# Search steps interleaved with other work, and expert gates in slabs of sixteen keys

## The chip, the cores and the metric

The kernel runs on one core of a Trainium2 chip. The metric is the device time of one execution in microseconds, lower is better. Three runs of the kernel before gave 3557.41, 3567.39 and 3569.17 us; the median is 3567.39.

## The reference, cut to what matters

The program is a two-layer model on 512 tokens of width 1024. Each layer has a mixer (an RWKV-7 half and an S5 half), a cross attention to 256 memory rows, and a PEER layer: a feed-forward layer with 16384 experts, of which each token takes 16 for each of 8 heads. The change touches the PEER layer alone:

```python
def peer_ffn(h, wq, keys, u_tab, v_tab):          # for each block of 128 tokens
    q = (hc @ wq).reshape(128, 8, 2, 128)
    sc = jnp.einsum('thcd,hckd->thck', q, keys)    # scores of 128 keys in each of 2 halves
    s1, i1 = lax.top_k(sc[:, :, 0], 16)
    s2, i2 = lax.top_k(sc[:, :, 1], 16)
    cand = s1[..., :, None] + s2[..., None, :]     # 256 pairs
    top, pos = lax.top_k(cand, 16)
    eidx = take(i1 * 128 + i2, pos)                # expert numbers
    gate = jax.nn.softmax(top, axis=-1)
    act = jax.nn.gelu(jnp.einsum('thkd,td->thk', u_tab[eidx], hc))
    return jnp.einsum('thk,thkd->td', gate * act, v_tab[eidx])
```

All data are float32.

## The kernel before, in words

`peer(pg, layer)` (L2358) treats 352 of the 512 tokens densely: it multiplies them with all 16384 rows of both expert tables, an up tile of 128 experts at a time, and weighs the results with a gate that is zero for experts that were not chosen. The other tokens go by gathering: 128 tokens on the 128 partitions, with 128 chosen experts each, plus 32 extra tokens of which each has four partitions and 32 chosen rows a partition. So GpSimd gathers 160 groups of 128 rows of the first table (512 KB each, `ROWS` = 160), VectorE takes the dot product of each with the tokens (a "row", L2881), and later 128 groups of the second table are added up, again one instruction of VectorE each.

A product in float32 is made of three products in a rounded format: ScalarE writes the high half of a tile (`split_high`, L216), VectorE the low half (`split_low`, L221), and `product` (L224) issues three matmuls for each of 8 planes, so 24 a tile. There are three buffers for raw tiles, three for high halves and three for low ones (`NRAW`, `NSPLIT`), so that ScalarE can make the high half of tile m only when the product of tile m - 3 is done, and SyncE's `load(m)` waits for the low half of tile m - 3.

The order of the tiles is `STREAM` (L2339): 144 of them, 16 query tiles of 512 columns (`q`) and 128 up tiles of 352 columns (`u`). Each engine runs its own list in order, and what stands ahead of an instruction on its engine holds it.

1. **Search**, eight slots, one a head. While TensorE does 12 tiles (10 up and the 2 query tiles of the next head) and the scores, VectorE runs `search(hd)` (L2892): two `top16` calls over 128 keys for two blocks of tokens and both halves, pair sums (`PAIRS`, 64 pairs that alone can be among the best 16), a third `top16` over them, arithmetic on the positions that finds which of the four groups of pairs a winner is in, masks (`hit`) that turn positions into key numbers, sums over them, and the row numbers that GpSimd waits for (`rows_found`). Steps that depend on one another on VectorE are joined by `link` (L95): the instruction increments a semaphore and the next one waits for it. At ten places of a slot, and twice more behind it, `split_and_row` puts one low half and, from the second head on, a row or two: 14 rows a slot (`ROWS_BY_HEAD`).
2. **Bridge**, six tiles, in which the gates are formed and transposed.
3. **Spreading**, 22 groups of 16 tokens with one or two up tiles each (`GROUP_AT`): VectorE makes one-hot matrices, TensorE multiplies them into dense gates, ScalarE copies them to `spill`, and `store_gates(n)` on SyncE (L2478) writes the 1 MB of a group to memory, laid out by slabs of `SLAB` = 8 keys, so in runs of 512 bytes. 0.75 rows a group.
4. **Tile loop**, the last 12 up tiles. VectorE has 135 low halves done when it enters its part of the loop (near L3085); each step is a low half and rows up to a count that grows by `ROWS_BY_TILE` = 2 a tile.
5. **Down**, 128 tiles of the second table. `weigh(e)` (L3091) multiplies the up results of a tile (kept in SBUF for the last 18 keys, else loaded back by `load_act`) with its gates from a slab, ScalarE and VectorE split both, TensorE multiplies. A slab (8 keys, 1408 KB) is loaded by one transfer, `load_slab(s)` (L2483), into one of two buffers. In the first 8 tiles (`DOTS_UNTIL`) VectorE finishes the rows of the first table that are left; the rows of the second table are spread over the later tiles. The order of the tiles is `DOWN`.

GpSimd issues the gathers (L2564) in the order `ROW_ORDER`, six buffers ahead of VectorE, and at the counts in `PART_GATES_AT` and `PART_GATHER_AT` the transfers for the extra tokens.

## Time and profile before

| what | value |
|---|---|
| median of 3 runs | 3567.39 us |
| profiled execution | 3566.76 us, its span 3564.8 us |
| TensorE busy | 3416.0 us, 96% of the span |
| VectorE busy | 2986.1 us, 84% |
| ScalarE busy | 1363.2 us, 38% |
| moved by DMA | 922.20 MB, mean 259 GB/s |

Busy time is the sum of an engine's instructions with overlaps counted once. The trace gives the start of each instruction; the distance between the starts of two tiles' first matmuls is what a tile really costs. "Granted clock" is the share of TensorE's full speed in a stretch.

### The profile page before, as it was taken

The page shows a single profiled execution, that of the slowest core. Times are in us where ns is not written, and L with a number is a line of the kernel's source. Part 1 is how long each engine was busy: PE and PEld are TensorE (multiplying, and loading weights), DVE is VectorE, ACT ScalarE, POOL GpSimd, SP SyncE. Part 2 cuts the span into 40 slices and gives each one's busy share as a digit, 9 for nine tenths or more (in the row PEclk, how much of TensorE's full clock was granted, in tenths as well). Part 3 has the DMA queues.
Part 4 walks back from the last instruction along what each step waited for, and adds up shares of the span by engine and source line. Part 5 has one row for each costly group of instructions (what it writes and reads, how often), then busy time and mean ns, then how long its engine had stood idle before and what let it go on. Part 6 is the DMA issues. An engine that isn't in the chain of part 4 may idle for free. (4 is left out here: it accounts for less than half of the span.)

```text
span 3564.8 us, 68150 instructions
## 1 busy us (share of the span) xinstructions
PE 3416.0 (96%) x27550; PEld 3116.0 (87%) x27550; DVE 2986.1 (84%) x5697; ACT 1363.2 (38%) x2116; POOL 989.6 (28%) x756
## 2 busy tenths in 40 slices
PE   8899899999999989999999989999999999999998
PEld 5678677999899989999997877789998999999997
DVE  8687575899999978888888757489999997888887
ACT  3541343433334433333344135343333443333333
POOL 2000000133343245445510000002334324543452
PEclk9999999999999999999999999999999999999999
DMA  7820431699899999999962043259989999999995
GB/s 236 302 95 23 132 113 60 192 292 310 291 358 319 345 336 359 369 376 368 366 220 83 20 121 119 65 155 299 311 297 348 317 349 327 374 383 384 363 367 205
DMA packets 392170, 922.20 MB, mean 259 GB/s; under 512 B 33968, under 2 KB 211248, under 8 KB 385072
## 3 DMA queue, kind: packets, MB, share of 16 engines
q1 hardware_dynamic: 298672, 582.20, 48.7%
q0 software_dynamic: 93184, 335.65, 25.1%
q8 instruction: 217, 3.56, 0.4%
q14 instruction: 97, 0.79, 0.1%
HBM read 802.51 MB, written 113.05 MB: 257 GB/s over the span
## 5 line engine op out<-in xcount | busy, mean ns | idle before, releaser
L2564 POOL DMA_INDIRECT row<-in_peer_u_rows,row_at x320 | 414.6, 1296 | 739.0 <-DVE row L2881 629.3
L228 PE MATMUL peer_ps<-peer_h_high,tile_high 128*128 128x352 f32 (+1 forms) x1504 | 498.0, 331 | 17.0 <-DVE tile_low L221 14.1
L229 PE MATMUL peer_ps<-peer_h_low,tile_high 128*128 128x352 f32 (+1 forms) x1504 | 492.2, 327 | 0.0
L230 PE MATMUL peer_ps<-peer_h_high,tile_low 128*128 128x352 f32 (+1 forms) x1504 | 491.7, 327 | 0.0
L221 DVE TENSOR_TENSOR tile_low<-peer_tile,tile_high 128x1024 fp32r<-128x1024 f32 x362 | 441.4, 1220 | 30.9 <-ACT tile_high L216 27.4
L228 PE MATMUL peer_ps<-gate_high,tile_high 128*128 128x352 f32 x1360 | 442.6, 325 | 9.6 <-DVE tile_low L221 9.3
L230 PE MATMUL peer_ps<-gate_high,tile_low 128*128 128x352 f32 x1360 | 441.3, 325 | 0.0
L229 PE MATMUL peer_ps<-gate_low,tile_high 128*128 128x352 f32 x1360 | 439.5, 323 | 0.0
L216 ACT ACTIVATE tile_high<-peer_tile 128x1024 fp32r<-128x1024 f32 x362 | 379.5, 1049 | 14.1 <-DMA peer_tile<-in_peer_u 14.1
L216 ACT ACTIVATE gate_high<-weighed 128x352 fp32r<-128x352 f32 x256 | 127.8, 499 | 643.6 <-DMA peer_tile<-in_peer_v 332.6
L2881 DVE SCALAR_TENSOR_TENSOR row<-row,h_own 128x1024 f32<-128x1024 f32 x256 | 307.4, 1219 | 23.1 <-DMA row<-in_peer_u_rows,row_at 22.9
L2716 ACT ACTIVATE up_act<-peer_ps 128x352 f32<-128x352 f32 x220 | 102.5, 466 | 575.6 <-PE peer_ps L230 294.1
L228 PEld LDWEIGHTS peer_ps<-peer_h_high,tile_high 128*128 128x128 f32 x1504 | 282.7, 188 | 38.7 <-DVE tile_low L221 23.8
L2564 POOL DMA_INDIRECT late_row<-in_peer_v,row_at x130 | 223.5, 1719 | 239.6 <-DVE h_own L2887 221.1
L230 PEld LDWEIGHTS peer_ps<-peer_h_high,tile_low 128*128 128x128 f32 x1504 | 283.2, 188 | 3.9
L229 PEld LDWEIGHTS peer_ps<-peer_h_low,tile_high 128*128 128x128 f32 x1504 | 283.1, 188 | 3.9
L2564 POOL DMA_INDIRECT row<-in_peer_v,row_at x126 | 215.7, 1712 | 216.3 <-DVE h_own L2887 201.7
L228 PEld LDWEIGHTS peer_ps<-gate_high,tile_high 128*128 128x128 f32 x1360 | 255.3, 188 | 16.0 <-DVE tile_low L221 15.4
L228 PE MATMUL peer_ps<-peer_h_high,peer_tile_high 128*128 128x352 f32 (+1 forms) x736 | 249.9, 339 | 18.0 <-DVE peer_tile_low L221 12.4
L230 PEld LDWEIGHTS peer_ps<-gate_high,tile_low 128*128 128x128 f32 x1360 | 256.3, 188 | 0.0
L229 PEld LDWEIGHTS peer_ps<-gate_low,tile_high 128*128 128x128 f32 x1360 | 255.6, 188 | 0.0
L221 DVE TENSOR_TENSOR gate_low<-weighed,gate_high 128x352 fp32r<-128x352 f32 x256 | 133.0, 520 | 135.2 <-ACT tile_high L216 92.6
(571 smaller groups left out, 8179.0 us busy)
## 6 DMA issues: line engine op xcount, KB each, us to landing
peer_tile<-in_peer_u SPq DMA_DIRECT2D x256, 512.0 KB, 5.4
peer_tile<-in_peer_v SPq DMA_DIRECT2D x256, 512.0 KB, 6.2
gates<-gates_out SPq DMA_DIRECT2D x44, 1024.0 KB, 9.1
gates_in<-gates SPq DMA_DIRECT2D x32, 1408.0 KB, 10.4
acts<-up_act SPq DMA_DIRECT2D x220, 176.0 KB, 5.6
act_in<-acts SPq DMA_DIRECT2D x220, 176.0 KB, 6.1
in_w<-in_w_in SPq DMA_DIRECT2D x32, 512.0 KB, 3.6
peer_tile<-in_peer_wq SPq DMA_DIRECT2D x32, 512.0 KB, 5.1
```

The source lines that it names most:

```text
L216: return act.activation(out, value, ACT.Copy)
L221: return dve.tensor_tensor(out, value, high.bitcast(F32), ALU.subtract)
L228: pe.matmul(out, wh, mh, start=first, stop=False)
L229: pe.matmul(out, wh, ml, start=False, stop=False)
L230: return pe.matmul(out, wl, mh, start=False, stop=last)
L2564: pool.indirect_dma_start(row_of(n)[:, :], None, table, bass.IndirectOffsetOnAxis(ap=row_at[:, row_col(n):row_col(n) + 1], axis=0)) \
L2716: act.activation(up[i % NUP][:, :], ps[m % NPS][:, 0:TD], ACT.Gelu_apprx_tanh).then_inc(taken.sem, 1)
L2881: last = dve.scalar_tensor_tensor(out=x, in0=x, scalar=1.0, in1=(h_own if j < OWN else h_extra)[:, :], op0=ALU.mult, op1=ALU.mult, accum_o ...
```

## The change

Five edits, all in `peer` and its constants.

- **Order of the search.** `link` gives way to `mark` (increment, and remember the count) and `until` (wait for a count). Between a producer and its consumer stands `gap(hd, share)`, which issues low halves and rows in step with its share of 29 (`GAPS`). In `top16` the four replaces go ahead of the four finds. The slot has the same 12 low halves (9 in the first) and 16 rows for 14.
- **Pairs.** `PAIRS` becomes (0,1,16), (1,2,8), (3,4,4), (7,8,2), (15,1,1): four groups of 16 and one of 1, 65 in all. The group number of a position is then a shift by 4 bits (`fours`, a constant buffer) in place of three comparisons and a cast.
- **Rows.** 16 a head, 0.75 a group, 1.5 a tile (2.0 before); the counts at which GpSimd issues the transfers for the extra tokens move with them.
- **Slabs.** `SLAB` is 16: stored runs are 1 KB. A slab has four pieces by token groups (`PIECES`: 6, 6, 5 and 5 groups of 16 tokens). The last sixteen keys are taken as two half slabs first (`TAKEN`), the other seven slabs whole. `PIECES_AT` says behind which tile load SyncE issues each piece. The second slab buffer lies over the plane `h_high` (address 41376), so its first load waits until all up products are done. The number of kept up results stays 18.
- **Rooms and waits.** `late_row3` moves to 208864, and GpSimd waits for all gate stores before the first gather of the second table.

```diff
-ROWS_BY_HEAD, ROWS_BY_GROUP, ROWS_BY_TILE = 14, 0.75, 2.0
+ROWS_BY_HEAD, ROWS_BY_GROUP, ROWS_BY_TILE = 16, 0.75, 1.5
-PAIRS = ((0, 1, 16), (1, 3, 8), (4, 4, 4), (8, 8, 1))
+PAIRS = ((0, 1, 16), (1, 2, 8), (3, 4, 4), (7, 8, 2), (15, 1, 1))
+GAPS = 29
-SLAB, NSLAB, NACT = 8, 2, 4
+SLAB, NSLAB, NACT = 16, 2, 4
+PIECES = ((0, 6), (6, 12), (12, 17), (17, TD // SPILL))
-KEPT_LATE, KEPT_EARLY = SLAB, 10
+KEPT_LATE, KEPT_EARLY = SLAB // 2, 10
+TAKEN = [(SLABS - 1, SLAB // 2, SLAB // 2), (SLABS - 1, 0, SLAB // 2), *((s, 0, SLAB) for s in (SLABS - 2, *range(SLABS - 2)))]
+PIECES_AT = [(0, 2, 4, 5), (4, 5, 6, 7), *([TAKEN_AT[s - 1] + 1 + j for j in ((2, 5, 8, 11) if TAKEN[s - 1][2] == SLAB else (0, 2, 4, 5))]
+                                           for s in range(2, len(TAKEN)))]
...
-        slabs = [buf(f"gates_in{b}", [P, TD // SPILL, SLAB * SPILL]) for b in range(NSLAB)]
+        slabs = [buf("gates_in0", [P, TD // SPILL, SLAB * SPILL]), pg.placed("gates_in1", [P, TD // SPILL, SLAB * SPILL], F32, 41376)]
...
-            def load_slab(s):
+            def load_slab(s, piece):
                 if s >= NSLAB:
-                    sp.wait_ge(weighed.sem, weighed.at(SLAB * (s - NSLAB + 1)))
+                    sp.wait_ge(weighed.sem, weighed.at(TAKEN_AT[s - NSLAB + 1]))
+                elif s:
+                    sp.wait_ge(summed.sem, summed.at(UPS))
                 else:
                     for b in range(2):
                         sp.wait_ge(gates_stored[b].sem, gates_stored[b].at(16 * ((TD // SPILL + 1 - b) // 2)))
-                sp.dma_start(slabs[s % NSLAB][:, :, :], gates[DOWN[s * SLAB] // SLAB]) \
+                (at, first, some), groups = TAKEN[s], slice(*PIECES[piece])
+                sp.dma_start(slabs[s % NSLAB][:, groups, 0:some * SPILL], gates[at][:, groups, first * SPILL:(first + some) * SPILL]) \
...
-                if m == GROUP_AT[GROUPS] + late + 1:
-                    load_slab(0)
-                if m == UPS:
-                    load_slab(1)
+                if m - GROUP_AT[GROUPS] - late - 1 in PIECES_AT[0]:
+                    load_slab(0, PIECES_AT[0].index(m - GROUP_AT[GROUPS] - late - 1))
...
                 if n == ROWS:
                     pool.wait_ge(summed.sem, summed.at(UPS))
+                    for b in range(2):
+                        pool.wait_ge(gates_stored[b].sem, gates_stored[b].at(16 * ((TD // SPILL + 1 - b) // 2)))
...
+            def mark(ins):
+                vec_step.n += 1
+                ins.then_inc(vec_step.sem, 1)
+                return vec_step.n
+            def until(step):
+                dve.wait_ge(vec_step.sem, step)
+            def lows_of(hd):
+                return BRIDGE + 3 - (PH - 1 - hd) * (UPS_HEAD + 2) - slot_start[0]
+            def gap(hd, share):
+                gaps_done[0] += share
+                some = ROWS_BY_HEAD if hd else 0
+                both = (lows_of(hd) + some) * gaps_done[0] // GAPS
+                own_lows = min(both, (2 * lows_of(hd) * gaps_done[0] + GAPS) // (2 * GAPS))
+                lows(slot_start[0] + own_lows - done[0])
                 if hd:
+                    rows((hd - 1) * ROWS_BY_HEAD + both - own_lows)
+            def top16(some, hd, shares):
                 for x, r, v, a in some:
                     last = dve.max(v[:, 0:8], x)
-                link(last)
+                best_8 = mark(last)
+                gap(hd, shares[0])
+                until(best_8)
+                for x, r, v, a in some:
+                    last = dve.match_replace(out=r, in_to_replace=v[:, 0:8], in_values=x, imm_value=LOWEST)
+                replaced = mark(last)
                 for x, r, v, a in some:
                     dve.max_index(a[:, 0:8], v[:, 0:8], x)
-                    last = dve.match_replace(out=r, in_to_replace=v[:, 0:8], in_values=x, imm_value=LOWEST)
-                link(last)
-                split_and_row(hd)
+                gap(hd, shares[1])
+                until(replaced)
                 for x, r, v, a in some:
                     last = dve.max(v[:, 8:16], r)
-                link(last)
+                next_8 = mark(last)
+                gap(hd, shares[2])
+                until(next_8)
...
-                link(dve.tensor_copy(spotf[0][:, :, :], pos[:, :, :]))
-                link(dve.tensor_scalar(spotf[1][:, :, :], spotf[0][:, :, :], float(PAIR_AT[1]), None, ALU.is_ge))
-                link(dve.scalar_tensor_tensor(out=spotf[1][:, :, :], in0=spotf[0][:, :, :], scalar=float(PAIR_AT[2]),
-                                              in1=spotf[1][:, :, :], op0=ALU.is_ge, op1=ALU.add))
-                for _ in range(2):
-                    link(dve.scalar_tensor_tensor(out=spotf[1][:, :, :], in0=spotf[0][:, :, :], scalar=float(PAIR_AT[3]),
-                                                  in1=spotf[1][:, :, :], op0=ALU.is_ge, op1=ALU.add))
-                link(dve.tensor_copy(wide[:, :, :], spotf[1][:, :, :]))
+                block_known = mark(dve.tensor_tensor(wide[:, :, :], pos[:, :, :], fours[:, :, :], ALU.logical_shift_right))
...
                 for into in hits:
+                    gap(hd, 1)
+                    until(hits_known)
```

The other joints of the search (the pair sums, the masks, the sums over them, the row numbers) change in the same way: `link(x)` becomes `mark(x)`, a `gap` and an `until`.

## Rows read from the trace of the kernel before

**Rows 1.** The page: busy us, share of the span, instructions of each engine.

```profile
PE 3416.0 (96%) x27550; PEld 3116.0 (87%) x27550; DVE 2986.1 (84%) x5697; ACT 1363.2 (38%) x2116; POOL 989.6 (28%) x756
```

**Rows 2.** Windows: length; busy PE, PEld, DVE, ACT, POOL; clock, DMA share, GB/s.

```profile
1092.79:1285.06 192.27, 191.88 (x1881) 181.32 (x1882) 182.28 (x186) 88.82 (x153) 54.54 (x34) 1.00 0.99 320
1285.06:1374.64 89.58, 75.85 (x434) 73.24 (x433) 76.08 (x118) 27.74 (x40) 58.79 (x41) 0.94 0.98 375
1374.64:1837.50 462.86, 456.18 (x2797) 452.02 (x2797) 390.21 (x479) 169.78 (x235) 220.74 (x122) 1.00 0.96 360
...
2988.04:3076.64 88.60, 75.79 (x434) 73.72 (x434) 75.42 (x118) 27.56 (x40) 60.36 (x41) 0.94 0.99 376
3076.64:3534.78 458.14, 456.09 (x2809) 454.25 (x2809) 394.34 (x480) 169.53 (x234) 201.16 (x122) 1.00 0.95 362
```

**Rows 3.** Windows of TensorE: layer 1's search slots, then an undisturbed down stretch.

```profile
2395.47:2446.61 51.14, 51.14 (x306) 1.00 0.93 311
2446.61:2501.14 54.53, 52.57 (x307) 1.00 0.89 291
...
2662.41:2717.62 55.21, 55.21 (x338) 1.00 0.95 327
2717.62:2762.02 44.40, 41.50 (x258) 1.00 0.99 376
...
3120.00:3400.00 280.00, 279.64 (x1728) 1.00 0.99 376
```

**Rows 4.** Windows of VectorE: two of its search slots of layer 1.

```profile
2448.16:2500.28 52.12, 51.12 (x165) 1.00 0.89 292
...
2609.13:2662.09 52.96, 51.89 (x168) 1.00 0.86 292
```

**Rows 5.** Timeline of VectorE in a search slot: start us, us, line, operation.

```profile
746.87 0.29 DVE L2852 FIND_INDEX8 key_at<-key_top,key_scores 128x8 uint32<-128x128 f32 x1
747.07 0.07 DVE L2853 MATCH_VALUE_LOAD key_rest<-key_top,key_scores 128x8 f32 x1
...
748.69 0.28 DVE L2853 MATCH_REPLACE8 key_rest<-key_top,key_scores 128x128 f32<-128x128 f32 x1
749.00 1.22 DVE L221 TENSOR_TENSOR peer_tile_low<-peer_tile,peer_tile_high 128x1024 fp32r<-128x1024 f32 x1
750.15 1.22 DVE L2881 SCALAR_TENSOR_TENSOR row<-row,h_own 128x1024 f32<-128x1024 f32 x1
...
778.36 0.18 DVE L2915 CAST spotf<-pos 128x64 bf16<-128x64 uint32 x1
...
780.53 0.68 DVE L2927 TENSOR_TENSOR hit<-spotf,pair_starts 128x1024 bf16<-128x1024 bf16 x1
```

**Rows 6.** Timelines of the hand-over in layer 0: VectorE, then TensorE.

```profile
1280.11 1.22 DVE L2881 SCALAR_TENSOR_TENSOR row<-row,h_own 128x1024 f32<-128x1024 f32 x1
...
1290.94 1.22 DVE L221 TENSOR_TENSOR tile_low<-peer_tile,tile_high 128x1024 fp32r<-128x1024 f32 x1
...
1335.61 0.52 DVE L3102 TENSOR_TENSOR weighed<-acts_kept,gates_in 128x352 f32<-128x352 f32 x1
...
1337.62 1.22 DVE L2881 SCALAR_TENSOR_TENSOR row<-row,h_own 128x1024 f32<-128x1024 f32 x1
...
1304.05 0.44 PE L228 MATMUL peer_ps<-peer_h_high,peer_tile_high 128*128 128x352 f32 x1 [3.26 <-DVE peer_tile_low L221]
```

**Rows 7.** DMA issues (KB, median us to landing); ACT's waits, layer 0's down stage.

```profile
peer_tile<-in_peer_v SPq DMA_DIRECT2D x256, 512.0 KB, 6.2
gates<-gates_out SPq DMA_DIRECT2D x44, 1024.0 KB, 9.1
gates_in<-gates SPq DMA_DIRECT2D x32, 1408.0 KB, 10.4
...
ACT gate_high L216 <- DMA peer_tile<-in_peer_v: 212.3, 72, 7.9
```

**Rows 8.** Waits of VectorE, layer 1's search slots: us, times, longest.

```profile
DVE row L2881 <- DMA row<-in_peer_u_rows,row_at: 2.4, 1, 2.4
```

More of the change, by code:

```diff
@@ L2519, in _ @@
                 load(UPS + e)
-                s = (e - NRAW) // SLAB + NSLAB
-                if (e - NRAW) % SLAB == SLAB - 1 and s < SLABS:
-                    load_slab(s)
+                for s in range(1, len(TAKEN)):
+                    if e in PIECES_AT[s]:
+                        load_slab(s, PIECES_AT[s].index(e))
                 if e in FIRST_LOADS and follows:
@@ L2929, in search @@
-                link(dve.tensor_tensor(hit[:, 1, :, :, :], across(spotf[1][:, :, :], TOPK), every(ranks[:, :, :]), ALU.is_equal))
+                paired = mark(last)
+                until(keys_found)
+                dve.sem_inc(searched.sem, 1)
+                dve.tensor_copy(at_first[:, :, :, :], twins(at[:, :, 0, :]))
+                cast = mark(dve.tensor_copy(payload[:, 1, :, :, :], twins(at[:, :, 1, :])))
+                gap(hd, 1)
+                until(paired)
+                pairs_found = top16([(cand[:, tb, :], rest[:, tb, 0:PAIRED], best[:, tb, own], pos[:, tb, :])
+                                     for tb in range(TB)], hd, (2, 1, 2))
@@ new lines, in search @@
+                until(block_known)
+                masked = mark(dve.tensor_tensor(spot[:, :, :], mask[:, :, :], wide[:, :, :], ALU.logical_shift_right))
+                until(spot_0)
+                dve.tensor_tensor(hit[:, 0, :, :, :], across(spotf[0][:, :, :], TOPK), every(starts[:, :, :]), ALU.is_ge)
+                until(masked)
+                spot_1 = mark(dve.tensor_tensor(spot[:, :, :], pos[:, :, :], spot[:, :, :], ALU.bitwise_and))
+                gap(hd, 1)
+                until(spot_1)
@@ L2930, in search @@
+                spot_1 = mark(dve.tensor_copy(spotf[1][:, :, :], spot[:, :, :]))
+                gap(hd, 1)
+                until(spot_1)
+                hit_1 = mark(dve.tensor_tensor(hit[:, 1, :, :, :], across(spotf[1][:, :, :], TOPK), every(ranks[:, :, :]), ALU.is_equal))
+                gap(hd, 1)
+                until(hit_1)
                 pairs = hit[:, :, :, :, :].rearrange("p j t a (k c) -> p (j t a) k c", c=2)
-                link(dve.tensor_tensor(pairs, pairs, payload[:, :, :, :, :].rearrange("p j t (a k) c -> p (j t a) k c", k=1)
-                                       .to_broadcast([P, 2 * TB * TOPK, TOPK // 2, 2]), ALU.mult))
@@ new lines, in search @@
+                until(hits_known)
+                chosen_known = mark(dve.tensor_tensor(chosen[:, :, 0:2, own], summed_hits[:, :, :, 0, :].rearrange("p j t k -> p t j k"),
+                                                      summed_hits[:, :, :, 1, :].rearrange("p j t k -> p t j k"), ALU.add))
+                gap(hd, 1)
+                until(chosen_known)
+                row_known = mark(dve.scalar_tensor_tensor(out=row_atf[:, :, :], in0=chosen[:, TB - 2:TB, 1, own], scalar=float(NKEY),
+                                                          in1=chosen[:, TB - 2:TB, 0, own], op0=ALU.mult, op1=ALU.add))
@@ L3057, in _ @@
                     shift_top(0)
-                for _ in range(BRIDGE + 3 - (PH - 1 - hd) * (UPS_HEAD + 2) - done[0]):
-                    split_and_row(hd)
-                rows(hd * ROWS_BY_HEAD)
                 if hd == BATCH:
```

69 lines of the change are left out of this document (30 added, 39 removed).

## The prediction, as it was put on record

> **What bounds the kernel now.** First the page's busy line: TensorE is busy for 96% of the span, VectorE for 84% [rows 1]. The reader should see that there is little idle TensorE time to win, so the question is in which stages TensorE runs below its own pace. I therefore read the busy times by stage, then TensorE alone over the seven search slots of the second layer, then the same on VectorE, and only then single instructions.
>
> TensorE's own pace: the undisturbed down stretch has 1728 matmuls in 280 us, 0.162 us each, so 3.89 us for a tile of 24 [rows 3]. A search slot is 10 up tiles, 2 query tiles and one set of scores; the first one runs without a gap and takes 51.14 us [rows 3], my floor for a slot. The next four take 54.53 us, then (three rows left out) 54.10, 53.59 and 53.58: 11.2 us above the floor. The sixth holds two extra sums and no idle time. The seventh has 10 tiles and one extra sum, but VectorE must do 12 halves meanwhile: 44.40 us against 10 x 3.84 (from start to start of undisturbed up tiles, not shown) + 2.0 (the sixth slot's 55.21 - 51.14, for two sums) = 40.4, so 4.0 over. That is 15 us a layer, and both layers take 366.55 us for these slots. VectorE is why: its slots are 52.12 and 52.96 us, all but about 1 us busy, and that 1 us is the sum of short gaps at dependent steps [rows 4]. So in slots two to five VectorE sets the pace and TensorE follows.
>
> The spreading stage is at TensorE's pace (191.88 busy of 192.27 us) and nothing is to be had there [rows 2]. The hand-over from up tiles to down tiles is where the pace is lost: 18 tiles take 89.58 us in layer 0 and 88.60 in layer 1 against 18 x 3.87 = 69.7, so 19.9 and 18.9 us, at a mean granted clock of 0.94 [rows 2]. The down stage from its tenth tile on is 117 tiles: 462.86 and 458.14 us against 455.0, so 7.9 and 3.1 us. In sum 30 (search) + 38.8 (hand-over) + 11 (down) = 80 us could be won at the very most.
>
> **Search slot, on VectorE.** (a) Waits. A find that lasts 0.29 us is followed 0.20 us later by the next load of match values, with no wait between; where a wait stands, the low half follows the 0.28 us replace only after 0.31 us [rows 5]. A wait right behind its producer thus costs 0.11 us. Of 29 of them a slot, 20 lie outside the index arithmetic (12 in the three top-16 calls, one behind the pair sums, seven in the hits and behind), and nearly all now have a low half or a row between: 28 such pieces go over 29 shares. Saved 20 x 0.11 = 2.2 us. (b) Index arithmetic. From the cast at 778.36 to the hit step at 780.53 are 2.17 us, ten instructions [rows 5]. Five steps (compare, three more, cast) become one shift; six short ones at about 0.13 to 0.16 us are left: saved 1.2 us. (c) A fifth pair step and 65 candidates for 64: +0.15. (d) 16 rows a slot for 14: a low half or a row starts 1.15 us after the one before [rows 5], +2.3 us. Sum -0.95 us a slot.
>
> VectorE's slot goes from 52.1 to 53.0 to 51.2 to 52.0, beside a floor of 51.14. I leave 0.7 us of excess in each of the four slots (2.8 for 11.2), and take 4.0 to about 3.9 in the seventh, since there 12 halves, 16 rows and more gathers meet transfers already at 376 GB/s and a DMA share of 0.99 [rows 3]; two gathers more are 1.05 MB, at 376 GB/s 2.8 us of transfers, against 1 us of VectorE saved. Gain 8.5 a layer, **17 us**. Bounds: if bursts were all of the excess, 15 a layer; if none of (a) comes, below zero (rival 1).
>
> Here the Trainium skill speaks against the change. VectorE: DVE Perf Modes (The DRAIN you can't avoid) says that a flush follows each operation whether a semaphore is there or not and that the semaphore costs nothing extra; its advice is to cut operations, not waits. The two starts of rows 5 disagree: 0.20 us without a wait and 0.31 with one. By that page (a) would be zero, and the slot 1.25 us longer for its two rows.
>
> **Hand-over.** Rows dotted by its start: 7 x 14 + 4 + 16 = 118 before, 7 x 16 + 4 + 16 = 132 after. VectorE enters the tile loop with 135 halves done, so the loop's first call catches up: int(2.0 x 4) = 8 rows at once before, int(1.5 x 4) = 6 after. Before, they run from 1280.11 and hold the next low half until 1290.94 [rows 6]: 10.8 us, of it 8 x 1.15 = 9.2 work and the rest gathers not yet landed. TensorE stands behind this half, and the tile load that waits for it starts late too. Six rows are the six buffers, already landed: 6.9 us, and the half starts at 1287.0 for 1290.94. Behind the burst each tile has 1.5 rows for 2, VectorE 1.15 + 1.7 = 2.9 us instead of 3.45 of 3.86. The first slab, 1408 KB in one transfer behind a tile load, landed in 10.4 us (median) against 6.2 for a tile [rows 7]; rows then came late, and TensorE stood 3.26 us at 1304.05 [rows 6]. Now four pieces of 320 or 384 KB come over six tiles. In the first eight down tiles 18 rows become 10: 2.0 (from the weighing at 1335.61 to the row at 1337.62 [rows 6]) + 2.25 x 1.15 = 4.6 us a tile, over 3.89, becomes 2.0 + 1.25 x 1.15 = 3.5, under it. The clock: 0.94 over 89.6 us is 5.4 us of lost full speed, part at 1.2 GHz behind the stalls; with shorter stalls most of it stays at 2.4.
>
> What is late next: the gelu of the dots, which ACT still waits for behind the eighth down tile's rows (that tile is 5.9 us long, 2 over); the first weighing with its two splits ahead of the first down product (2 us); and the last pieces of the first two slabs. Those are issued at tiles 144 and 7, behind the low half of three tiles earlier, and wanted two tiles and a row later: 2 x 3.89 + 1.2 = 9 us, where tile loads land in 6.2. SP passes its wait for the gate stores as before, ahead of piece one, and the second slab's for the last up product, at most a tile, with loads queued behind it. I leave 9 us of 19.9 and 18.9: **gain 21**. Bounds: 0 (rival 2) to 33 (3 us left a layer).
>
> **Down stage.** The bytes are the same; each eighth tile one 1408 KB transfer held the tile loads up (ACT waited 212.3 us for them in layer 0, at the longest 7.9, of which TensorE felt 7.9) [rows 2, 7]. Now 640 or 768 KB at each third tile. Demand in such a stretch is 512 + 512 + 176 + 235 KB a tile of 3.89 us, 378 GB/s, and 376 were carried at full pace [rows 3]. I leave 4 of 11: **gain 7** (bounds -4 to 11). The 44 gate stores go from 512 byte to 1 KB runs; landing may go from their 9.1 us to anything between a tile's 6.2 and a slab's 10.4 [rows 7]. The spreading stage hides it, at TensorE's pace with ACT busy for 88.8 of 192.3 us [rows 2]: nothing; without the cover 22 x 1.3 us a layer. The memset, the two waits more on POOL (both long met) and moved buffers: nothing, beside the work of other engines; uncovered under 1 us.
>
> DMA: Bandwidth & Descriptors (Bandwidth) of the Trainium skill advises transfers of 1 MiB or more, against the split. This trace carries 376 GB/s with tile loads of 512 KB as the bulk, so I take no loss; by the page the pieces would cost part of the 7.
>
> **Sum.** 3566.8 (the profiled execution: 3564.8 of span and 2.0 around it; 0.6 under the median of 3567.4) - 17 - 21 - 7 = **3522 us**.
>
> **Rivals.** (1) Taking the waits away brings VectorE nothing: low halves and rows in the gaps let the next dependent step start no earlier than now. Then the two extra rows lengthen the slot, -1.2 + 0.15 + 2.3 = +1.25 us in five slots of each layer, +12.5; 3567 + 12.5 - 28 = 3551. Against it stand the starts of rows 5, though they show it for short steps alone. The Trainium skill's page VectorE: DVE Perf Modes (The DRAIN you can't avoid) is for it, as quoted. (2) Hand-over bound by the first slabs: their last pieces arrive later than 9 us, VectorE stands, then TensorE, and the clock falls as it does now; the stalls change their name and gain 0: 3543. For it: the DMA share is 0.98 [rows 2], and half slabs are read in runs of 512 bytes out of a slab of sixteen; against: a piece is a quarter of 1408 KB. (3) Slower: a row in nearly every gap holds the search behind its gather. VectorE runs in order, so each wait lengthens the slot. The search slots of layer 1 run at a DMA share of 0.85 to 0.99 [rows 3] and get two gathers more. At w us a row the slot is 51.6 + 16w; ten slots at w = 0.5 give 59.6 against 53.95, +56, less the 28 of the other two: 3595. It decides from w = 0.32, where 10 x (51.6 + 16w - 53.95) is 28. Against: in these slots VectorE waited for a gather once, 2.4 us [rows 8], 0.02 us a row.
>
> **Chances.** Forecast 0.60, rival 2 0.20, rival 1 0.13, rival 3 0.05, something else 0.02. The likeliest alone is 3505 to 3537; 8 in 10 with the rivals 1 and 2 taken in: 3500 to 3552. Beyond 0.3% (10.7 us, about what this kernel's runs differ by) faster: 0.88; within 0.3%: 0.07, the upper part of rival 1 and half-failed gains; slower 0.05.
>
> **What would show it.** Slots two to five of the search at 51.2 to 52.2 us on TensorE and 51 to 52 on VectorE; no replace-to-low gap of 0.31; six rows in one go before the tile loop; 18 tiles of the hand-over near 79 us with a clock of 0.97 or more; no period of eight tiles in TensorE's gaps. Wrong if slots stay over 53, if VectorE's weighing waits for the gates, or if rows wait for gathers in the search.

## The result

| | median us | runs | ratio to the kernel before |
|---|---|---|---|
| before | 3564.4 | 3557.4 to 3569.2 (4) | |
| after | 3513.7 | 3507.7 to 3530.2 (4) | 0.987 [0.984, 0.990] |
| after, once more | 3518.35 | 3514.2 to 3527.0 (4) | 0.9873 [0.9854, 0.9893] |

The forecast was 3522 us, with a range of 3500 to 3552. The change makes the kernel 1.3% faster. The two profiles of the changed kernel are of its runs of 3530.23 us ("after") and 3514.24 us ("the repeat"); where they differ, both are given.

TensorE's tile starts cut a layer into stages. Sums of both layers, in us (search is slots one to seven; hand-over is the last ten up tiles and the first nine down tiles, one up tile more than the 18 tiles of [rows 2]; down is the 117 tiles behind them):

| kernel | search | bridge | spreading | hand-over | down |
|---|---|---|---|---|---|
| before | 733.1 | 50.6 | 394.2 | 185.9 | 922.9 |
| after | 722.2 | 60.3 | 395.3 | 161.9 | 909.0 |
| after, repeat | 717.0 | 56.0 | 394.3 | 165.9 | 909.0 |
| predicted change | -17 | 0 | 0 | -21 | -7 |
| measured, repeat | -16.1 | +5.4 | +0.1 | -20.0 | -13.9 |

The down stage of layer 0 before ends later than in [rows 2]: that window stops at 1837.50 with 2797 matmuls in it, 13 short of 117 tiles, and the tile starts give 464.80 us for 462.86.

```profile
1374.64:1839.44 464.80, 458.12 (x2810) 453.96 (x2809) 392.15 (x481) 170.49 (x235) 220.74 (x122) 1.00 0.95 358
```

These five columns hold 44.5 us of the 52.3 between the spans of before (3564.8) and of the repeat (3512.5). The other 7.8 lie outside these stages: that remainder is 1278.1 before, 1279.8 after, 1270.3 in the repeat and 1272.2 to 1279.1 in the eleven other profiles below. The two profiles of one kernel span nearly the whole range, so nothing is read from it.

The page of after, its first line (it answers [rows 1]): TensorE has lost 12 us of busy time, VectorE 37. Of TensorE's 12 us, 8.5 are lost in the 18 tiles of the two hand-overs (151.6 busy in [rows 2], 143.2 below), whose granted clock went from 0.94 to 1.00 and 0.98.

```profile
PE 3404.2 (96%) x27550; PEld 3114.2 (88%) x27550; DVE 2949.2 (84%) x5651; ACT 1362.5 (39%) x2116; POOL 885.3 (25%) x756
```

Windows of after, columns as in [rows 2]: 18 tiles of the hand-over (nine up, nine down) and the 117 of the down stage, in each layer. The reader should see 77.1 us where 89.6 and 88.6 stood [rows 2], and a down stage with TensorE busy in all of it. In the repeat the 18 tiles take 78.6 and 79.5 us.

```profile
1289.10:1366.22 77.12, 70.72 (x434) 69.53 (x433) 59.63 (x90) 27.44 (x40) 35.73 (x27) 1.00 0.97 349
1366.22:1820.70 454.48, 454.48 (x2810) 454.48 (x2809) 396.20 (x481) 170.46 (x235) 160.10 (x122) 1.00 0.96 365
...
2966.70:3043.75 77.05, 72.43 (x434) 71.01 (x434) 59.62 (x90) 27.33 (x40) 35.02 (x27) 0.98 0.97 352
3043.75:3498.22 454.47, 454.47 (x2810) 454.47 (x2809) 395.99 (x480) 169.51 (x234) 155.57 (x122) 1.00 0.96 362
```

TensorE alone in layer 1's search slots (answers [rows 3]). Slots two to five were 54.53 to 53.58 and are 51.17 to 54.30: near the floor of 51.14 at first, above it later; the fifth is over the 53 us that the prediction named as a sign of being wrong (53.35 in the repeat). The seventh went from 44.40 to 42.87.

```profile
2376.55:2427.69 51.14, 51.14 (x306) 1.00 0.94 332
2427.69:2478.86 51.17, 51.17 (x306) 1.00 0.92 323
2478.86:2530.54 51.68, 51.52 (x307) 1.00 0.97 346
2530.54:2582.79 52.25, 51.77 (x305) 1.00 0.93 328
2582.79:2637.09 54.30, 52.31 (x305) 1.00 0.90 310
...
2692.41:2735.28 42.87, 41.87 (x258) 1.00 0.99 375
```

Timeline of VectorE in after (answers [rows 5]): behind the last replace the next operation of the search now starts 0.19 us later, where 0.31 us passed before, since the wait between them is gone. Further on is the burst ahead of the tile loop (answers [rows 6]), six rows in 6.87 us for eight in 10.8.

```profile
747.85 0.27 DVE L2879 MATCH_REPLACE8 key_rest<-key_top,key_scores 128x128 f32<-128x128 f32 x1
748.04 0.07 DVE L2882 MATCH_VALUE_LOAD key_at<-key_top,key_scores 128x8 f32 x1
...
1284.17 1.22 DVE L2912 SCALAR_TENSOR_TENSOR row<-row,h_own 128x1024 f32<-128x1024 f32 x1
...
1291.04 1.22 DVE L221 TENSOR_TENSOR tile_low<-peer_tile,tile_high 128x1024 fp32r<-128x1024 f32 x1
```

DMA issues of after, then two waits in layer 0's hand-over and one in its down stage (the last answers [rows 7]; us, times, longest). The gate stores land as before, 9.2 us for 9.1, with runs twice as long. ScalarE's wait for down tiles fell from 212.3 to 57.9 us. New are VectorE's waits for a slab in the hand-over. ScalarE's longest wait for an up tile there is 7.4 us, for 5.2 before.

```profile
gates<-gates_out SPq DMA_DIRECT2D x44, 1024.0 KB, 9.2
...
gates_in<-gates SPq DMA_DIRECT2D x28, 768.0 KB, 7.8
gates_in<-gates SPq DMA_DIRECT2D x28, 640.0 KB, 8.9
```
```profile
ACT tile_high L216 <- DMA peer_tile<-in_peer_u: 10.0, 3, 7.4
...
DVE weighed L3145 <- DMA gates_in<-gates: 5.6, 2, 4.4
...
ACT gate_high L216 <- DMA peer_tile<-in_peer_v: 57.9, 23, 5.8
```

The place that the prediction did not look at is the bridge. Windows of the two bridges of after, then VectorE's timeline in the first: 30 us for 25.3, at a clock of 0.98 and 0.94. Four rows of the last head wait 6.1 us for their gathers, and no low half is made for 12.4 us (1073.26, not shown, to 1085.66).

```profile
1057.20:1086.94 29.74, 24.61 (x154) 24.04 (x154) 20.03 (x41) 15.23 (x24) 13.24 (x15) 0.98 0.92 322
2735.28:2765.82 30.54, 26.19 (x153) 25.61 (x153) 20.59 (x42) 14.26 (x24) 14.95 (x15) 0.94 0.92 322
```
```profile
1076.07 1.23 DVE L2912 SCALAR_TENSOR_TENSOR row<-row,h_extra 128x1024 f32<-128x1024 f32 x1 [1.39 <-DMA row<-in_peer_u_rows,row_at]
...
1079.88 1.22 DVE L2912 SCALAR_TENSOR_TENSOR row<-row,h_extra 128x1024 f32<-128x1024 f32 x1 [2.58 <-DMA row<-in_peer_u_rows,row_at]
...
1085.66 1.22 DVE L221 TENSOR_TENSOR peer_tile_low<-peer_tile,peer_tile_high 128x1024 fp32r<-128x1024 f32 x1
```

### The profile page after: what moved, and what is told of

It is laid out like the page before. It is cut to its first block and busy times, and to the rows that moved or that the text cites. A ratio compares the mean times of both kernels' runs of the same rounds, so it can differ in the third digit from the quotient of the medians.

```text
span 3528.5 us, 68006 instructions
## 1 busy us (share of the span) xinstructions
PE 3404.2 (96%) x27550; PEld 3114.2 (88%) x27550; DVE 2949.2 (84%) x5651; ACT 1362.5 (39%) x2116; POOL 885.3 (25%) x756
## 3 DMA queue, kind: packets, MB, share of 16 engines
q0 software_dynamic: 93184, 335.65, 25.3%
## 5 line engine op out<-in xcount | busy, mean ns | idle before, releaser
L228 PE MATMUL peer_ps<-peer_h_high,tile_high 128*128 128x352 f32 (+1 forms) x1504 | 499.2, 332 | 20.0 <-ACT up_act L2726 10.9
L229 PE MATMUL peer_ps<-peer_h_low,peer_tile_high 128*128 128x352 f32 (+1 forms) x736 | 245.1, 333 | 0.0
L230 PE MATMUL peer_ps<-peer_h_high,peer_tile_low 128*128 128x352 f32 (+1 forms) x736 | 244.9, 333 | 0.0
L2574 POOL DMA_INDIRECT row<-in_peer_v,row_at x126 | 168.8, 1340 | 279.2 <-DVE h_own L2918 251.7
```

What stands on the lines that cost most here:

```text
L228: pe.matmul(out, wh, mh, start=first, stop=False)
L229: pe.matmul(out, wh, ml, start=False, stop=False)
L230: return pe.matmul(out, wl, mh, start=False, stop=last)
L2574: pool.indirect_dma_start(row_of(n)[:, :], None, table, bass.IndirectOffsetOnAxis(ap=row_at[:, row_col(n):row_col(n) + 1], axis=0)) \
```

## The experiments

Each edits the changed kernel. Stage times, sums of both layers in us (a profile each), and medians:

| run | search | bridge | spreading | hand-over | down | median | ratio to before |
|---|---|---|---|---|---|---|---|
| after, repeat | 717.0 | 56.0 | 394.3 | 165.9 | 909.0 | 3518.4 | 0.9873 |
| waits at once | 753.3 | 59.1 | 395.2 | 165.0 | 909.0 | 3560.1 | 0.9982 |
| old search | 759.7 | 51.5 | 394.0 | 162.4 | 909.0 | 3553.6 | 0.9975 |
| rates of before | 705.0 | 53.7 | 394.3 | 200.6 | 908.9 | 3538.1 | 0.9920 |
| one transfer a slab | 719.0 | 56.8 | 394.4 | 174.7 | 938.2 | 3562.7 | 0.9984 |
| slabs of 8 | 721.6 | 57.0 | 394.5 | 154.2 | 912.2 | 3519.8 | 0.9897 |
| early stores | 705.0 | 66.9 | 394.3 | 165.9 | 909.0 | 3512.7 | 0.9864 |
| rows behind the numbers | 715.9 | 65.4 | 394.2 | 161.6 | 909.1 | 3526.5 | 0.9900 |
| low halves first | 718.1 | 52.2 | 405.8 | 164.5 | 909.0 | 3526.4 | 0.9879 |
| both of these two: stores, low halves | 704.7 | 57.8 | 406.0 | 160.4 | 909.2 | 3519.4 | 0.9868 |
| the same with slabs of 8 | 705.9 | 53.2 | 405.1 | 155.6 | 920.0 | 3515.0 | 0.9846 |
| early stores, slabs of 8 in halves | 705.2 | 61.7 | 394.9 | 152.1 | 909.0 | 3500.8 | 0.9819 |

The intervals of the ratios reach 0.0014 to 0.0036 to either side.

**The repeat.** No edit.

> The changed kernel once more, nothing edited: the anchor for the other kernels of this call. Every theory expects 3508 to 3520 us (the four runs so far: 3507.7 to 3530.2, median 3513.7), and the same stage times as in its first profile: search 363 and 359 us in the two layers, bridge 30 and 30.5, spreading 198 and 197, hand-over 81, down stage 454.5. If the profile of the first look was the slow one by a stage of its own, that stage is shorter here; if not, the difference is spread.

It came as expected. The search is 5 us shorter than in the first profile and the bridge 4; two executions of one kernel differ by that much in a stage, and since every other row of the table is one profile too, smaller differences in a stage are not read as effects.

**The waits paid at once.**

```diff
             def mark(ins):
                 vec_step.n += 1
                 ins.then_inc(vec_step.sem, 1)
+                dve.wait_ge(vec_step.sem, vec_step.n)
                 return vec_step.n
```

> Keeps the changed search order, its 16 rows and its gaps, but VectorE now waits for each marked step right behind it, before the gap's splits and rows instead of behind them (about 25 waits a slot). Theory A (my step (a)): each wait that a step pays at once costs VectorE 0.11 us, so a slot's VectorE time grows by 2.2 to 2.8 us, from about 51.5 to 54; the first slots, now at TensorE's 51.14, come back to 53.5 to 54.5 and the search stage grows by 8 to 17 us in the sum of two layers: 3522 to 3531 against 3514 of the changed kernel. Rival 1 (an instruction behind another one pays the same with or without the wait): VectorE's slot does not change by more than 0.5 us, and the time stays within 3 us of the changed kernel. A third reading: what matters was only that the gathers' rows are spread evenly (the gaps are kept here); then also nothing changes.

Measured +42 us, nearly the whole gain, with 36.3 of it in the search, where Theory A had 8 to 17. Here is VectorE's timeline of this run at the same place as above: 0.31 us from the replace to the next operation, for 0.19.

```profile
747.66 0.28 DVE L2880 MATCH_REPLACE8 key_rest<-key_top,key_scores 128x128 f32<-128x128 f32 x1
747.97 0.09 DVE L2883 MATCH_VALUE_LOAD key_at<-key_top,key_scores 128x8 f32 x1
```

VectorE's windows over the same slot (the fifth of layer 1) follow, for the repeat, for this run and for the run with the old search, one each (length, busy time with instructions, clock, DMA share, GB/s).

```profile
2568.97:2621.68 52.71, 51.30 (x170) 1.00 0.91 311
```
```profile
2604.26:2659.18 54.92, 53.78 (x169) 1.00 0.89 296
```
```profile
2604.49:2659.77 55.28, 54.21 (x173) 1.00 0.90 297
```

The run has 336 instructions more than the repeat, all of them waits of VectorE, 21 in each of 16 slots. Busy time grew by 2.48 us, 0.118 us a wait. Theory A had the price right (0.11), and rival 1 falls; so does the third reading. What A had wrong is the conversion into TensorE's time: with VectorE busy for over 51.14 us a slot, twelve of the 14 slots grow by 2.0 to 4.5 us (3.1 on average), where I had let a quarter to a half of VectorE's 2.5 come through. The two sixth slots, with their two extra sums, do not grow. Why the twelve grow by more than 2.5 was not tried.

**The old search.** `search`, `top16`, `split_and_row`, `PAIRS` and the filling of a slot as before, with 16 rows a head.

> The changed kernel with the search order of before alone: four pair steps and the index arithmetic as before, its linked waits, the splits and rows in clumps between them, the filling of a slot behind the search; 16 rows a head are kept. Theory: the linked waits cost VectorE 0.12 us each and the longer index arithmetic about 1.2 us a slot; VectorE's busy time was 2.2 to 2.7 us a slot higher with all waits paid at once, and that run's search took 377 and 376 us against 359 and 358. So this one takes 372 to 380 a layer (before: 366.5 with 14 rows, and two more rows a slot add 1.2 us each), and the bridge goes back to 25.3, 2.5 us a layer less, because the last head's row numbers are known 8 us earlier: 3538 to 3555. Rival: the clumps did the harm, not the waits: then it is above the run with the waits paid at once (search over 380).

Search 380.6 and 379.1 (expected 372 to 380), bridge 51.5, time 3553.6. It is 6.4 us of search above the run that pays its waits, so the evener order and the shorter index arithmetic together bring 0.5 us a slot (0.43 of VectorE's busy time in the slot shown), and the waits 2.5 of busy time. The two were not separated. The bridge gives back 4.5 us: that cost belongs to the new search. Two rows more a slot cost 759.7 - 733.1 = 26.6 us, 1.9 a slot, in the old order, and 717.0 - 705.0 = 12 us in the new one.

**The rates of before.**

```diff
-ROWS_BY_HEAD, ROWS_BY_GROUP, ROWS_BY_TILE = 16, 0.75, 1.5
+ROWS_BY_HEAD, ROWS_BY_GROUP, ROWS_BY_TILE = 14, 0.75, 2.0
-PART_GATES_AT = (71, 119)
+PART_GATES_AT = (63, 105)
```
(and `PART_GATHER_AT` as before)

> Undoes the row rates alone: 14 rows a head in the search instead of 16, 2.0 instead of 1.5 rows a tile in the hand-over, with the other places of the partial gates that belong to them. Theory: the hand-over's gain came from the shorter burst of rows there (8 rows in 10.8 us before, 6 in 6.9 after), so its first part (from the first tile of 134 to 144) comes back by 15 to 22 us over both layers; the search gets back 2.3 us of VectorE a slot, of which TensorE sees less than 1 us a slot because the stores hold it (gain 2 to 5 us in the sum), and the bridge stands as it is. Together 3524 to 3533 us. Rival: the hand-over's gain came from the first slabs arriving in parts, not from the rows: then the hand-over stays within 5 us of 81 a layer, and the time is 3510 to 3516.

The theory holds in kind, but its sizes and the forecast of 3524 to 3533 (measured 3538.1) missed: the hand-over is 34.7 us longer for 15 to 22, the search 12 shorter for 2 to 5. TensorE's windows of the hand-over in layer 0, in this run and in the repeat: the slower clock is there too.

```profile
1267.90:1319.17 51.27, 43.61 (x242) 0.90 0.98 356
1319.17:1366.81 47.64, 39.62 (x216) 0.93 0.99 359
```
```profile
1270.24:1315.24 45.00, 40.59 (x242) 0.96 0.97 346
1315.24:1352.70 37.46, 35.48 (x218) 1.00 0.94 331
```

Note that 200.6 is above the 185.9 of the kernel before, which has these rates too: something else in the change makes the hand-over worse.

**One transfer a slab.** `PIECES = ((0, TD // SPILL),)`, at the place of the first piece.

> Keeps slabs of 16 keys and their 1 KB runs, but loads each slab by one transfer of 2.8 MB instead of four. Theory: the split is what smooths the queue in the down stage. With one transfer, the u, v and activation tiles queue behind it; the stall with which the down stage of the kernel before was marked every slab comes back and doubles in size as the slab is doubled, while its count is halved: 5 to 9 slabs a layer at 1.5 to 2.5 us, +15 to +35 us in all, and the hand-over's own two first slabs come later too, +5 to +10: 3534 to 3560. Rival: 16 keys and 1 KB runs made the gain of the down stage; then it stays within 2 us of 454.5 a layer and only the hand-over changes: 3512 to 3524.

Down stage 468.3 and 469.9, with 1 to 5 us lost within two tiles at each slab load (the tenth and the twentieth down tile, then every sixteenth). The time, 3562.7, is just over the forecast of 3534 to 3560. First its window in layer 0, then ScalarE's wait for down tiles in it (after: 57.9 us).

```profile
1365.12:1833.41 468.29, 458.85 (x2810) 455.67 (x2809) 396.07 (x482) 171.89 (x237) 186.60 (x122) 1.00 0.95 352
```
```profile
ACT gate_high L216 <- DMA peer_tile<-in_peer_v: 123.3, 39, 8.5
```

The theory holds: with one transfer a slab, 16 keys are slower than the 8 of before (938.2 us for 922.9), and the split makes them good.

**Slabs of 8.** All of the slab edit undone (8 keys, 512 byte runs, 1408 KB in one transfer, the old buffers and places); search and rates stay.

> The changed search and rates, but the slabs as before: 8 keys, stored in 512 B runs, each loaded by one transfer of 1.4 MB, with the late row buffer and the places of the loads as before. Together with the run that kept 16 keys and took the split away (down stage 468.3 and 469.9, against 454.5 with the split) it tells which part of the slab edit brings what. Theory: the split is the whole gain of the down stage, and 16 keys without it cost more than 8 keys: the down stage comes back to 459 to 463 a layer (+10 to +17 in the sum), the spreading stays at 189.4 for its first 30 tiles since TensorE hides the stores there at a DMA share of 0.98 instead of 0.94, and the hand-over is within 4 us a layer of the changed kernel's 82.5: 3528 to 3542. Rival: 1 KB runs matter, the stores with 512 B runs take the queue from the tile loads: then spreading or hand-over grow by more than 5 us a layer and the time is 3545 or more.

The forecast of 3528 to 3542 missed: 3519.8, hardly to be told from the changed kernel. The down stage lost only 3.2 us, and the hand-over, in which I expected no difference, was 11.7 us shorter. TensorE's windows of the hand-over in layer 0:

```profile
1280.35:1321.00 40.65, 39.06 (x241) 1.00 0.97 373
1321.00:1356.38 35.38, 35.27 (x219) 1.00 0.98 379
```

So there are four cases of the hand-over: rates and slabs of before 185.9, rates of before and new slabs 200.6, new rates and slabs of before 154.2, both new 165.9. (The first has the old search too, which the run with it shows to be worth 3.5 us here at most; after and its repeat differ by 4.0.) The rates bring 32 to 35 us, the slab edit costs 12 to 15. Rival 2 was half right. In the repeat TensorE waits 6.3 us in layer 0's hand-over and 7.0 in layer 1's for low halves, and with the old slabs 1.6 and 3.0. In layer 0 VectorE stands before it because an up tile lands late (6.04 us, behind ScalarE's high half). In layer 1 it stands for a piece of the slab, just as rival 2 says, and TensorE's first down tile is 5.9 us late behind it:

```profile
2986.51 0.96 DVE L3145 TENSOR_TENSOR weighed<-acts_kept,gates_in 128x352 f32<-128x352 f32 x2 [4.61 <-DMA gates_in<-gates]
```

With slabs of 8 VectorE waits for no slab in either hand-over, and neither does it in the last run below, which issues its first slab in two parts between up tiles. So it is not that parts stand between up tiles. What is left is that there are four and the last goes out five tiles behind the first, that half slabs are read out of a slab of sixteen, or that the second buffer must wait for the up products; none of these was tried alone.

**Early stores.** SyncE issues `store(m - 5)` with tile m for `store(m - 6)`.

> The changed kernel, but SyncE issues each activation store one tile earlier in its program (five tiles behind the load it stands with, not six). In the search the rest above TensorE's floor of 51.14 us a slot is in slots where ScalarE's copy out of PSUM waits for the store from one of three buffers (141.9 of its idle time in the first layer's search of the repeat). Theory A: this wait is what holds the slots above the floor; a tile earlier takes it away, the six free slots come to 51.14 to 51.5 and the search shrinks by 5 to 12 us in the sum of the layers: 3506 to 3513 beside 3518 of the repeat. Rival (supported by the run with 14 rows, where the slots were at the floor and VectorE had 48.3 instead of 50.5 us of work a slot): the rest is VectorE's, the wait on the store is spare time; then nothing changes (3514 to 3521), or SyncE, waiting on a later activation, issues the tile loads later and it gets slower by up to 10 us.

ScalarE's waits in layer 0's search, six slots, in the repeat and in this run:

```profile
ACT up_act L2726 <- DMA acts<-up_act: 98.0, 30, 6.8
```
```profile
ACT up_act L2726 <- DMA acts<-up_act: 0.7, 1, 0.7
```

Theory A holds for the search: slots two to five are 51.12 to 51.95, and it is 12 us shorter. So what the changed kernel has left over the floor goes away with the wait for this ring of three buffers, while VectorE's work of 50.6 to 51.3 us a slot stays. It also goes away, to the same 705.0 us, with two rows fewer a slot, although over half of the wait is still there in that run, in the same six slots:

```profile
ACT up_act L2726 <- DMA acts<-up_act: 58.8, 17, 6.4
```

The excess thus needs both, a late ring and a VectorE with hardly any time to spare, and relieving either is enough. But 10.9 of the 12 us come back in the bridge, where TensorE now arrives earlier and the row numbers do not: at the end of layer 0's search VectorE stands 4.9 us for the gathers of two rows.

**Rows behind the numbers.** Five of the last head's 16 rows are done behind its search.

> The changed kernel, but 5 of the last head's 16 rows of work are moved from inside its search to behind the step that makes its row numbers; nothing else moves. In the changed kernel these numbers come 8 us later than before, so the first rows of the bridge wait for their gathers (6.1 us in all) and TensorE stands 3.3 us there, with its clock down behind that. Theory A: with 5 rows between, the gathers land before they are wanted; row numbers come 5 to 6 us earlier, the last search slot and the bridge together fall from 71.6 and 70.9 to about 68 (L0) and 68 (L1): 3511 to 3514 beside 3518 of the repeat, 4 to 7 us less. Rival: the rows only change places with the waiting, VectorE is the bound of that stretch by its work, and bridge and last slot stay within 1 us of the repeat.

There is no gain: last slot and bridge take 73.1 us in both layers, for 71.6 and 70.9 in the repeat and 72.9 and 73.4 in the first profile. The four rows no longer wait, but VectorE then stands 4.8 us before its next low half, so the rival's picture holds, that the rows only change places with waiting.

**Low halves first.** In the bridge:

```diff
-            rows(searched_rows + 4)
             dve.wait_ge(flip_taken.sem, flip_taken.at(TB - 1))
             lows(2)
+            rows(searched_rows + 4)
             share_gates()
```

> The changed kernel, but in the bridge VectorE makes the two low parts that follow before the four h_extra rows of the last head, not behind them. In the repeat these four rows wait 5.0 us in all for their gathers (issued from 1057.69, behind the row numbers at 1052.47 and the 5 us transfer that places them), no low part is made for 10.1 us, and TensorE takes 27.8 and 28.1 us for six tiles that took 25.3 before. Theory: TensorE gets its two tiles while the gathers land; the bridge comes down to 25.3 to 25.8 a layer, with 5 us less in the sum of both layers: 3511 to 3515 beside 3518.4 and 3513.7 of the two runs of the changed kernel. Rival (as with the 5 rows moved behind the row numbers, which gained nothing): the stretch is bound by the number chain and the spreading starts with the gates anyway, so what the bridge wins the first tiles of the spreading lose; no change within 2 us.

The rival is right that the spreading loses what the bridge wins, and more: the bridge is 3.8 us shorter, the spreading 11.5 us longer. VectorE's timeline shows why. From its last gates to the next low half it waits 7.54 us until ScalarE has taken the transposed gates; the four rows had filled this wait, and now hold up the spreading's first steps.

```profile
1064.12 0.22 DVE L3005 TENSOR_TENSOR own_gates<-best,total 128x64 f32<-128x64 f32 x1
...
1073.21 1.22 DVE L221 TENSOR_TENSOR peer_tile_low<-peer_tile,peer_tile_high 128x1024 fp32r<-128x1024 f32 x1 [7.54 <-ACT gate_row L2809]
```

So two things that the search hands on bind the bridge. One is a chain: pairs known, gates, transposes, about 9 us from the last gates on. These gates stand 15.9 us behind the bridge's start in after and 15.2 in the repeat, for 13.8 before (layer 0), so only 1.4 to 2.1 us later. The other is the row numbers, since the search now fills its slot to the end: 8.0 us behind the bridge's start in after and 7.2 in the repeat, where they came 1.6 ahead of it before (1065.18 beside 1057.20, and 1056.99 beside 1058.62). Their gathers, and so the four rows, now end later than the chain does.

**Both, and both with slabs of 8.**

> The changed kernel with both: the activation stores one tile earlier on SyncE, and the two low parts before the four rows in the bridge. The earlier stores alone brought the searches to the floor (352.7 and 352.3 against 359.0 and 358.0), but the bridge grew to 33.3 and 33.7, since TensorE came there sooner and the row numbers of the last head did not: the numbers' chain was then the bound. Theory: with the low parts first the bridge loses most of that, 25.5 to 28 a layer: 3512.7 less 11 to 15 us: 3498 to 3502. Rival: the row numbers bound the start of the spreading whatever TensorE does in between (gates can't be spread before they are known): then search and bridge together stay at 386 a layer and the time at 3511 to 3514.

> As the run with both, and the slabs of before (8 keys, 512 B runs, one transfer each). Alone, the slabs of 8 made the hand-over 76.0 and 78.2 against 82.5 and 83.4, and the down stage 456.8 and 455.4 against 454.5. Theory: the two add up: 8 us less than the run with both, 3490 to 3494. Rival: the stalls of 0.4 to 2.3 us that the kernel before has every eight tiles of its down stage come back, as TensorE is further ahead (down stage 458 to 463): then it is at or above the run with both.

Both forecasts missed. In the first the spreading again took 11.7 us more, which is the rival's mechanism, though not its numbers: search and bridge together are 381 and 382 us a layer for its 386, and the time is 3519.4, over its 3514. In the second the hand-over came down from 160.4 to 155.6, but stalls of 0.2 to 2.1 us returned at about every eighth down tile, from the fiftieth on in layer 0 and the 75th in layer 1: 459.0 and 461.0. That is the second rival's mechanism; the time, 3515.0, is 4 us under the run with both.

**Early stores, slabs of 8 in two transfers each.** The bridge as in the changed kernel. The constants against those of the run with slabs of 8:

```diff
-PIECES = ((0, TD // SPILL),)
+PIECES = ((0, 11), (11, TD // SPILL))
-PIECES_AT = [(0,), (), *((TAKEN_AT[s - 1] + NRAW - 1,) for s in ...)]
+PIECES_AT = [(0, 1), (), *((TAKEN_AT[s - 1] + NRAW - 1, TAKEN_AT[s - 1] + NRAW + 2) for s in ...)]
```

> The changed search and rates with the activation stores one tile earlier on SyncE, the bridge in the changed kernel's order, and slabs of 8 keys as before, each loaded by two transfers of 0.7 MB three tiles apart instead of one of 1.4 MB. What is open is which part of the slab edit keeps the down stage at its floor: the run with slabs of 8 in one transfer and the same early stores had stalls every eight tiles (459.0 and 461.0 a layer); slabs of 16 in four transfers had none (454.5), slabs of 16 in one transfer 468.3 and 469.9. Theory: it is the size of a transfer alone, so with 0.7 MB the stalls go: down stage 454.5 to 455.5 a layer, while the hand-over keeps the 78 us of the slabs of 8 and the search its floor of 352.5; against the run of early stores alone (3512.7) that is 8 to 10 us less: 3502 to 3506, the fastest of all. Rival: the number of packets of 512 B matters, or half as many slabs: then the down stage stays at 457 to 461 and the time at 3509 to 3516.

3500.8 us, 0.9819 [0.9802, 0.9835] of the kernel before, with the interval just below that of the changed kernel (0.9835 beside 0.9837). Windows: hand-over and down stage of layer 0, then the down stage of layer 1; behind them the slab loads of this run, which land in 7.3 us for 10.4 in one transfer [rows 7].

```profile
1277.48:1353.44 75.96, 74.49 (x458) 73.39 (x457) 64.38 (x100) 29.19 (x42) 39.19 (x28) 1.00 0.98 372
1353.44:1807.92 454.48, 454.48 (x2810) 454.48 (x2809) 396.51 (x479) 170.44 (x235) 140.10 (x122) 1.00 0.97 364
...
3015.91:3470.39 454.48, 454.48 (x2810) 454.48 (x2809) 395.79 (x478) 169.46 (x234) 148.07 (x122) 1.00 0.96 362
```
```profile
gates_in<-gates SPq DMA_DIRECT2D x64, 704.0 KB, 7.3
```

So 512 byte runs and 8 keys leave no stall in the down stage when a slab is split; neither the longer runs nor the larger slab is needed. Whether it is the size of a transfer or the three tiles between its halves was not separated.

## Why the prediction came out, step by step

- **What bounds the kernel: right in place, part wrong in cause.** VectorE bound search slots two to five, as said; once it was relieved, the remaining excess there (0.7 us a slot predicted, 1.0 in the repeat) needed a second cause, ScalarE waiting for activation stores, which the prediction never priced.
- **(a) 20 waits at 0.11 us = 2.2: right.** Measured 21 waits at 0.118, 2.5 us a slot. **(b), (c) index arithmetic and pair step, -1.05 net: too much**; about 0.5, with the evener order in it. **(d) two rows, +2.3: near**, 1.9 where VectorE is the bound. In sum VectorE's slot was to fall by 0.95 us; its busy time fell by 0.6, from 51.12 and 51.89 [rows 4] to 50.56 and 51.30 (VectorE's second slot in the line below, its fifth in the line of the repeat above). TensorE's search gained 16.1 (10.9 in the first profile) for 17, so its sum came out with terms that were off on both sides.

```profile
2424.17:2475.12 50.95, 50.56 (x165) 1.00 0.96 337
```

- **Bridge: the step that is missing.** It cost 5.4 us (9.7 in the first profile). I had costed what the gaps do to the search's length and not what they do to its end: an even spread puts the last result at the end of the slot, and in the last slot VectorE itself waits for the rows that it brings.
- **Spreading, 0: right**, 394.3 for 394.2. The longer runs of the gate stores changed nothing that can be seen (394.5 with 512 byte runs).
- **Hand-over, 21: right in sum (20.0 and 24.0), mis-sized in both its terms, the rows and the slabs.** The rates were worth 32 to 35 us, near the upper bound of 33 that I had given, and rival 2's mechanism, to which I gave a chance of 0.20 as an alternative, was there beside them: the slab edit took 12 to 15, part of it through VectorE's waits for a slab. The burst was as predicted (6.87 us for 6.9). The pieces of the first slabs did come late: VectorE waited 5.6 and 4.9 us for them in the first profile.
- **Down, 7: too small for the profile (13.9), too large for the edit.** The start was misread too: layer 0's window ended half a tile early, so 12.9 us were to be won and not 11. No period is left. But the old slabs lose only 3.2 us in the changed kernel and 10.8 in the version with early stores and low halves first; the loss from 1408 KB in one transfer varies between 3 and 14 us with what surrounds it. Part of the 13.9 therefore is not the slab edit's alone, and why it varies stays open.
- **Rivals.** (1) fell: with the waits paid at once the gain was gone. The Trainium skill's page VectorE: DVE Perf Modes (The DRAIN you can't avoid) measured that a semaphore costs nothing extra in a chain of copies. By that this run would have been no slower, and it was 42 us slower. (3) fell: VectorE waited for a gather once in layer 1's search slots, 0.6 us.

The total owes something to luck, since errors cancel: bridge +5 against down -7, and 11 to 14 us too little for the rates against 12 to 15 left out for the slabs. Of the 52.3 us between the two spans, the 7.8 outside the stages can't be told from scatter.

## What to carry to other kernels

Put independent work between a producer and the step that waits for it, and check where the chain's last result is wanted: spread evenly, a chain ends as late as its slot, so its last instance may want to be dense. (The old, denser order gives 4.5 us of the bridge back; a new order for the last head alone was not tried, and five of its rows moved behind its search gained nothing.) Price an engine's relief only up to the next limit, and look for that limit in the waits of the other engines (here a ring of three store buffers, beside a VectorE with little time to spare). When a large transfer shares a queue with small ones that are wanted on time, try a split before a new layout; here the layout cost 12 to 15 us elsewhere, and two spaced halves in the old layout were enough.

## What the runs showed of the hardware

- A wait on VectorE for its own step right before costs 0.12 us over going on with independent work (0.31 us for 0.19 from start to start; 2.48 us for 21).
- Halves of 704 KB beat whole transfers of 1408 KB in the down stage, 909.0 for 920.0 us over both layers (these runs differ in the order of the bridge too, and the halves stand three tiles apart), at the same bytes and a DMA share of 0.95 to 0.97. DMA: Bandwidth & Descriptors (Bandwidth) of the Trainium skill advises 1 MiB or more; here, with a queue shared by loads that others wait for, the measurement decides against it.
- TensorE's matmuls run at the lower clock for a while after a stall. In after, layer 0, the bridge ends with a stall of 3.3 us; then the first matmul takes 0.66 us and the 18 behind it 0.49, against 0.32 before the stall and from 1092.9 on. The granted clock of this stretch is 0.50, the lower of its two levels:

```profile
1086.94:1092.68 5.74, 5.74 (x20) 0.50 1.00 346
```

The bridges of the early stores, with stalls of 5.5 and 6.6 us in them, have a mean granted clock of 0.90.
